# Rotary queries of two heads from one weight slot, and attention scores from split operands

## The chip, the cores and the metric

One core of a Trainium2 chip runs the whole program. The metric is the device time of one execution in microseconds; lower is better. The median of three runs of the kernel before is 3111.38 us (3108.11 to 3111.99).

## The reference, cut to what matters

Two transformer blocks run on 512 tokens of width 1024. The first has two layers (a feed-forward part, a mixing part, a second feed-forward part, a gated projection), the second has one. The change touches only the attention branch of the mixing part of the first block, which has 8 heads in each of the 2 layers:

```python
q = (rmsnorm(q_c, q_norm_g) @ w_uq).reshape(b, s, 8, 128 + 64)     # from 384 columns
q_nope, q_rope = q[..., :128], apply_rope(q[..., 128:], cos, sin)
kv = (rmsnorm(kv_c, kv_norm_g) @ w_ukv).reshape(b, s, 8, 128 + 128) # from 256 columns
k_rope = apply_rope(k_r, cos, sin)                                  # one for all heads
# apply_rope: [x1*cos - x2*sin, x2*cos + x1*sin], halves of 32
# for each block of 128 queries, keys up to its end:
s = (q_nope @ k_nope.T + q_rope @ k_rope.T) * 192 ** -0.5           # chunk mask of 64
o = softmax(s) @ v
```

## The kernel before, in words

Activations lie transposed: features on the 128 partitions, the 512 tokens along the row. Every projection is cut into *weight slots*. A slot holds the weights for 128 output features, in K row tiles of 128x128; its result fills one of four PSUM banks (`proj`). PE reaches nearly full precision at the fast rate by splitting both operands into a rounded part and a remainder (`hi`, `lo`, type fp32r) and multiplying hi x hi, hi x lo and lo x hi, so a slot costs 3K matmuls of 512 columns (`three`, L1042 to L1044; `slot_mm`). Each slot passes four engines: SP loads it into `raw`, ACT rounds it (`split_hi`, L617), DVE subtracts (`split_lo`, L1477), PE multiplies, and DVE or ACT evacuates the bank. The splits run `AHEAD` = 2 slots ahead; the ring has `RING` = 4 places. Semaphores count slots: `slot_done` by PE, `slot_read` by whoever evacuates; PE may refill a bank once `slot_read` has reached it.

The order of work on each engine is written out by hand, and each engine works in its program order; PE's order is the one in which slots are numbered. In a layer the stages are: feed-forward, `lora` (6 slots), `conv` (12), `gates` (12), `head0` (the 4 slots of head 0), `gates_end` (4), `heads` (4 slots for each of heads 1 to 7), `branch_out`, `mix_out`, feed-forward, `ple`.

A head has four slots: content queries (K = 3), rotary queries (K = 3), keys (K = 2), values (K = 2). The weights of the rotary slot hold the 64 rotary columns twice, the second time with swapped halves; DVE multiplies its bank by a table of cosines and sines (`cs`), and the fold of the two halves is done in the keys' rotary operand `work(15)`, so that a contraction over 128 rows gives the rotated product. DVE copies the other three banks (`head_evac`, L1596 and L1598).

The period of a head, `core`, has the attention of head n and the slots of head n+1 interleaved. PE does: `turn(3)` (transposes of the probabilities, 4 tiles), `scores(1)`, slot 0, `turn(2)`, `scores(0)`, slot 1, `turn(1)`, slots 2 and 3, `turn(0)`; then `enter` for head n+1 (`scores(3)`, `scores(2)`, four transposes of v), then the product with v (`ot`, L1161). `scores(qt)` makes one block of 128 queries against (qt+1) x 128 keys: a plain f32 matmul for content (L1110), an fp32r matmul of 128 columns that adds the chunk mask (L1111), a plain f32 one for the rotary part (L1112). The trace records a plain f32 matmul as two. DVE takes the row maximum (L1606) and scales it (L1609), ACT takes the exponential with the row sum (`exp`, L679), DVE scales the row by the sum's reciprocal (`row_norm`, L1615 and L1618), PE transposes it (`turn`, L1122), ACT copies it (`copy_pt`, L707). At the end ACT and DVE split the head's output (L701, L1654). Head 7 has the first four slots of `branch_out` in place of a next head's. `enter` waits first for `slot_read` to reach the next head's last slot less one, later for the last one itself. GpSimd is idle in this stage; its sums of squares (`squares`, L530 to L535) come in the stages around it.

Of the kernel before, what the change touches and what calls it, by code (L numbers as in the profile page):

```python
# [26 lines left out]
P = 128  # L27
# [39 lines left out]
HEAD_TILES = [Q_LORA // P, Q_LORA // P, KV_LORA // P, KV_LORA // P]  # L67
_stage("gates", [KD] * 12)
_stage("head0", HEAD_TILES)
_stage("gates_end", [KD] * 4)  # L70
_stage("heads", HEAD_TILES * (HEADS - 1))
# [72 lines left out]
def build(nc, I, out_t):  # L144
    ctx = ExitStack()
    with ctx:
# [35 lines left out]
        work_t, _ = place("work", 16 * S)  # L182
        sq_t, _ = place("sq", S)
        acc_t, _ = place("acc", S)
        rs_t, _ = place("rs", S)
# [15 lines left out]
        vec0 = modc[:, 0:KD]  # L201
        small2 = stat_t[:, 32:64]
# [70 lines left out]
        v_turned, v_ready = sem("v_turned"), sem("v_ready")  # L273
# [118 lines left out]
        def _(sp):  # L392
# [51 lines left out]
            with sp.Fori(0, DEPTH) as layer:  # L444
# [6 lines left out]
                def head(s0, i):  # L451
                    for j in range(2):
                        load(Slot(layer, s0 + j, i, 4), I["head_q"][layer, (i if s0 == STAGE["head0"] else i + 1) * 2 + j])
                    for j in range(2):
                        load(Slot(layer, s0 + 2 + j, i, 4), I["head_kv"][layer, (i if s0 == STAGE["head0"] else i + 1) * 2 + j])
                head(STAGE["head0"], 0)
                loads(layer, "gates_end", 4, lambda i: I["in_w"][layer, i + 30])
                with sp.Fori(0, HEADS - 1) as i:
                    head(STAGE["heads"], i)
# [41 lines left out]
        def _(pool):  # L501
# [7 lines left out]
            pool.memset(cmask[0:64, 64:P], NEG).then_inc(consts_ready, 1)  # L509
# [103 lines left out]
        def _(act):  # L613
# [96 lines left out]
            with act.Fori(0, DEPTH) as layer:  # L710
# [10 lines left out]
                for j in range(12):  # L721
# [8 lines left out]
                    if j >= 3 and j < 8:  # L730
                        act.wait_ge(lora_norm, 5 * layer + j - 2)
                        act.activation(a_hi(j - 3), work(j - 3), ACT.Copy).then_inc(lora_hi, 1)
                    if j % 3 == 2:
# [24 lines left out]
                s0 = STAGE["heads"] + AHEAD  # L758

                def heads(it):  # L760
                    end = isinstance(it, int)
                    for q in range(2):
                        core(layer, 2 * it + q, [Slot(layer, s0 + 4 * q + j + (24 if end else 0), 0 if end else it, 8) for j in range(4)],
                             end and q == 1)
                with act.Fori(0, HEADS // 2 - 1) as it:
                    heads(it)
                heads(HEADS // 2 - 1)
# [272 lines left out]
        def _(pe):  # L1040
# [65 lines left out]
            def scores(n, q, qt):  # L1106
# [33 lines left out]
            def core(layer, hd, q, slots, end):  # L1140
# [10 lines left out]
                if not end:  # L1151
                    run[3]()
# [1153 lines left out]
```

## Time and profile before

| | |
|---|---|
| median of 3 runs | 3111.38 us (3108.11 to 3111.99) |
| the profiled execution | 3112.69 us, of which the span from first to last instruction is 3110.9 |
| PE busy | 3043.7 us, 98% of the span, 13548 matmuls |
| PE weight load busy | 2449.6 us |
| DVE busy | 1725.1 us, 55% |
| ACT busy | 1058.1 us, 34% |
| GpSimd busy | 291.2 us, 9% |
| mean granted TensorE clock | 0.989 |

Busy shares are over the whole span. A matmul's duration holds the latency of the pipeline, and consecutive ones overlap, so what a matmul costs is read from the distance of starts. ACT's and DVE's operations overlap a little as well. The rows for the stage of the heads stand in the section on rows.

### The profile page before, as it was taken

The page shows a single profiled execution, that of the slowest core. Times are in us where ns is not written, and L with a number is a line of the kernel's source. Part 1 is how long each engine was busy: PE and PEld are TensorE (multiplying, and loading weights), DVE is VectorE, ACT ScalarE, POOL GpSimd, SP SyncE. Part 2 cuts the span into 40 slices and gives each one's busy share as a digit, 9 for nine tenths or more (in the row PEclk, how much of TensorE's full clock was granted, in tenths as well). Part 3 has the DMA queues.
Part 4 walks back from the last instruction along what each step waited for, and adds up shares of the span by engine and source line. Part 5 has one row for each costly group of instructions (what it writes and reads, how often), then busy time and mean ns, then how long its engine had stood idle before and what let it go on. Part 6 is the DMA issues. An engine that isn't in the chain of part 4 may idle for free. (4 is left out here: it accounts for less than half of the span.)

```text
span 3110.9 us, 39289 instructions
## 1 busy us (share of the span) xinstructions
PE 3043.7 (98%) x13548; PEld 2449.6 (79%) x13548; DVE 1725.1 (55%) x2469; ACT 1058.1 (34%) x1628; POOL 291.2 (9%) x236
## 2 busy tenths in 40 slices
PE   7999999999999999999999999999999799989999
PEld 6888888778888887888878877888888675678887
DVE  6555564565655556555456465555556767453334
ACT  4222323332332235322232333232223545552223
POOL 1000200000200023000020000200003214600000
PEclk9999999999999999999999999999999899999999
DMA  5232222113323222432232212333222420112222
GB/s 185 88 143 96 94 95 77 61 52 116 142 95 138 99 84 87 152 139 95 88 107 83 78 42 80 110 144 135 99 88 86 149 75 21 37 65 97 100 94 81
DMA packets 87965, 303.18 MB, mean 97 GB/s; under 512 B 10400, under 2 KB 20768, under 8 KB 86688
## 3 DMA queue, kind: packets, MB, share of 16 engines
q1 hardware_dynamic: 87840, 301.59, 27.7%
q8 instruction: 69, 1.13, 0.1%
q14 instruction: 56, 0.46, 0.0%
HBM read 299.45 MB, written 2.10 MB: 97 GB/s over the span
## 5 line engine op out<-in xcount | busy, mean ns | idle before, releaser
L1042 PE MATMUL proj<-u_hi,w_hi 128*128 128x512 f32 x2616 | 1029.2, 393 | 29.0 <-DVE u_lo L1482 23.0
L1043 PE MATMUL proj<-u_lo,w_hi 128*128 128x512 f32 x2616 | 1020.8, 390 | 0.0
L1044 PE MATMUL proj<-u_hi,w_lo 128*128 128x512 f32 x2616 | 1020.8, 390 | 0.0
L1477 DVE TENSOR_TENSOR w_lo<-raw,w_hi 128x1024 fp32r<-128x1024 f32 (+4 forms) x575 | 659.1, 1149 | 487.5 <-ACT w_hi L617 479.7
L617 ACT ACTIVATE w_hi<-raw 128x1024 fp32r<-128x1024 f32 (+4 forms) x575 | 538.7, 948 | 357.8 <-PE proj L1044 233.5
L1042 PEld LDWEIGHTS proj<-u_hi,w_hi 128*128 128x128 f32 x2616 | 492.7, 188 | 141.8 <-DVE u_lo L1482 28.5
L1043 PEld LDWEIGHTS proj<-u_lo,w_hi 128*128 128x128 f32 x2616 | 493.1, 188 | 104.4 <-issue 3.4
L1044 PEld LDWEIGHTS proj<-u_hi,w_lo 128*128 128x128 f32 x2616 | 492.9, 188 | 103.0
L1042 PE MATMUL proj<-a_hi,w_hi 128*128 128x512 f32 x960 | 380.8, 397 | 1.6 <-DVE a_lo L1787 0.9
L1044 PE MATMUL proj<-a_hi,w_lo 128*128 128x512 f32 x960 | 374.3, 390 | 0.0
L1043 PE MATMUL proj<-a_lo,w_hi 128*128 128x512 f32 x960 | 373.8, 389 | 0.0
L1493 DVE TENSOR_TENSOR work<-proj,rs 128x512 f32<-128x512 f32 x260 | 179.4, 690 | 304.3 <-PE proj L1044 304.1
L1042 PEld LDWEIGHTS proj<-a_hi,w_hi 128*128 128x128 f32 x960 | 180.3, 188 | 41.0 <-issue 2.6
L1044 PEld LDWEIGHTS proj<-a_hi,w_lo 128*128 128x128 f32 x960 | 180.2, 188 | 38.2
L1043 PEld LDWEIGHTS proj<-a_lo,w_hi 128*128 128x128 f32 x960 | 180.4, 188 | 36.1
L659 ACT ACTIVATE a_hi<-work 128x512 f32 (+1 forms) x88 | 55.6, 632 | 441.4 <-DVE work L1548 441.4
L530 POOL TENSOR_TENSOR acc<-h 128x512 f32<-128x512 f32 x6 | 6.2, 1040 | 2088.7 <-DVE h L1566 1321.3
L1566 DVE SCALAR_TENSOR_TENSOR h<-proj,h 128x512 f32<-128x512 f32 x96 | 66.3, 690 | 165.6 <-PE proj L1044 165.4
L656 ACT ACTIVATE work<-work 128x512 f32<-128x512 f32 x88 | 55.6, 632 | 266.0 <-DVE work L1493 266.0
L1551 DVE TENSOR_TENSOR a_lo<-work,a_hi 128x512 f32 (+1 forms) x88 | 61.0, 693 | 80.9 <-ACT a_hi L659 80.9
L623 ACT ACTIVATE u_hi<-h,vec 128x512 fp32r<-128x512 f32 x48 | 34.8, 725 | 141.2 <-DVE h L1566 82.2
L535 POOL TENSOR_TENSOR acc<-acc,sq 128x512 f32<-128x512 f32 x42 | 67.6, 1609 | 3.3
(410 smaller groups left out, 2826.7 us busy)
## 6 DMA issues: line engine op xcount, KB each, us to landing
raw<-in_ffn_gu SPq DMA_DIRECT2D x174, 512.0 KB, 3.5
raw<-in_in_w SPq DMA_DIRECT2D x68, 512.0 KB, 3.5
raw<-in_ffn_dn SPq DMA_DIRECT2D x64, 512.0 KB, 3.5
raw<-in_ff SPq DMA_DIRECT2D x64, 512.0 KB, 3.5
gate<-in_ada SPq DMA_DIRECT2D x8, 3072.0 KB, 11.5
raw<-in_ffn_dn SPq DMA_DIRECT2D x32, 384.0 KB, 3.0
raw<-in_in SPq DMA_DIRECT2D x18, 512.0 KB, 3.5
raw<-in_mla_out SPq DMA_DIRECT2D x16, 512.0 KB, 3.5
```

The lines of the kernel that those rows point to most:

```text
L535: pool.tensor_tensor(acc, acc, sq, ALU.add).then_inc(sum_ready, 1)
L617: act.activation(wt(w_hi, slot, slot.tiles), wt(raw, slot, slot.tiles), ACT.Copy)\
L623: act.activation(u_hi(m), h(m), ACT.Copy, scale=gain[:, m:m + 1]).then_inc(u_hi_ready, 1)
L656: act.activation(work(2 + q), work(q), ACT.Tanh, scale=0.5).then_inc(tanh_ready, 1)
L659: act.activation(a_hi_t[:, bass.ds((2 * it + q) * S, S)], work(8 + q), ACT.Copy)\
L1042: pe.matmul(out, w_h, x_h, start=first, stop=False)
L1043: pe.matmul(out, w_h, x_l, start=False, stop=False)
L1044: return pe.matmul(out, w_l, x_h, start=False, stop=last)
L1477: dve.tensor_tensor(wt(w_lo, slot, slot.tiles), wt(raw, slot, slot.tiles), wt(w_hi, slot, slot.tiles).bitcast(F32), ALU.subtract).then_inc ...
L1493: return dve.tensor_tensor(dst, proj[:, slot.pos, :], rs, ALU.mult)
L1551: dve.tensor_tensor(a_lo_t[:, at], work(8 + q), a_hi_t[:, at].bitcast(F32), ALU.subtract)\
L1566: dve.scalar_tensor_tensor(at, proj[:, slot.pos, :], 0.25, at, ALU.mult, ALU.add)\
```

## The change

Rotary weights are laid out with the 64 rotary columns of two heads side by side, once, in a new array `head_r`, and a slot of kind `r` gives the rotary queries of a pair. It comes with the slots of heads 0, 2, 4 and 6 (`HEAD_SLOTS`, `CORE_SLOTS`): in `head0`, and in the periods of heads 0, 2 and 4, which so have 4 slots, the others 3. The rotation is done after the projection. ACT copies the bank in four pieces of 32 rows with the halves of each head exchanged (`head_slot`, kind `r`); DVE multiplies the bank by the cosines; GpSimd multiplies the exchanged copy by the sines and adds the two. In the next period (for the first pair, in `gates_end`) ACT rounds one head's 64 rows of it and DVE writes the remainder into the other 64 rows of the same tile (`rot_hi`, `rot_lo`), once for each head of the pair.

Content queries and keys are split as they leave the bank: ACT writes the rounded part, DVE the remainder. ACT, no longer DVE, copies v. Keys carry the factor -192**-0.5, so the sign of the scores is turned: DVE takes the row minimum and no longer scales it, and the mask's constant changes sign. The rotary keys are split as well, after the last `conv` slot and no longer after its second. Scores are six fp32r matmuls: three for content, the mask, one rotary matmul over 128 rows (both parts of the queries stacked, against rounded keys) and one over 64 rows (rounded queries against the keys' remainder). `row_norm(0)` and the evacuation of the third slot change places on DVE. The loops over pairs of heads are written out on all engines. Places change: cosines and sines of all 128 rows lie in `acc` and `sq`, the rounded queries of odd heads in `rs`.

```diff
-HEAD_TILES = [Q_LORA // P, Q_LORA // P, KV_LORA // P, KV_LORA // P]
+HEAD_SLOTS = [("r", 0), ("q", 0), ("k", 0), ("v", 0)]
+CORE_SLOTS = [[("q", hd + 1), ("k", hd + 1)] + ([("r", hd // 2 + 1)] if hd in (0, 2, 4) else []) + [("v", hd + 1)]
+              for hd in range(HEADS - 1)]
+CORE_AT = [sum(len(c) for c in CORE_SLOTS[:hd]) for hd in range(HEADS)]
+HEAD_TILES = {"r": Q_LORA // P, "q": Q_LORA // P, "k": KV_LORA // P, "v": KV_LORA // P}
...
+        q_hi, q_lo = (lambda q: rs_r[:, :] if q else split_tile(0)), (lambda q: u_lo(7) if q else split_tile(8))
+        k_hi, k_lo = split_tile(4), split_tile(5)
+        kr_hi, kr_lo = split_tile(15), split_tile(1)
+        rot_q = lambda q: split_tile(2 + q)
+        v_tok = lambda q: ux(7) if q else work(7)
+        cos2, sin2 = acc, sq
+        turned_q = lambda p: (ux(6), ux(14)) if p else (work(11), work(12))
+        hi_rows = lambda q: slice(64 * q, 64 * q + 64)
+        lo_rows = lambda q: slice(64 - 64 * q, 128 - 64 * q)
+        ROT = 10
...
+                    if e == 1:
+                        for p in range(HEADS // 2):
+                            straight, crossed = turned_q(p)
+                            step = ROT * (HEADS // 2 * layer + p)
+                            pool.wait_ge(rope_step, step + 4)
+                            pool.tensor_tensor(crossed, crossed, sin2, ALU.mult).then_inc(rope_step, 1)
+                            pool.wait_ge(slot_read, Slot(layer, STAGE["heads"] + CORE_AT[2 * p - 2] + 2 if p else STAGE["head0"]).done)
+                            pool.wait_ge(rope_step, step + 5)
+                            pool.tensor_tensor(straight, straight, crossed, ALU.add).then_inc(rope_step, 1)
...
-                               ACT.Exp, bias=stat_t[:, 8 + qt:9 + qt], scale=SCALE1,
+                               ACT.Exp, bias=stat_t[:, 8 + qt:9 + qt], scale=-1.0,
                                accum_out=stat_t[:, 16 + qt:17 + qt]).then_inc(exp_ready, 1)
 
-            def core(layer, hd, slots, end):
+            def head_slot(layer, slot, kind, i):
+                q = i % 2
+                if kind == "v":
+                    act.wait_ge(slot_read, slot.done - 1)
+                act.wait_ge(slot_done, slot.done)
+                bank = proj[:, slot.pos, :]
+                if kind == "q":
+                    act.activation(q_hi(q), bank, ACT.Copy).then_inc(qk_hi_ready, 1)
+                elif kind == "k":
+                    act.activation(k_hi, bank, ACT.Copy, scale=-SCALE1).then_inc(qk_hi_ready, 1)
+                elif kind == "v":
+                    act.activation(work(6), bank, ACT.Copy).then_inc(slot_read, 1)
+                else:
+                    for r in range(4):
+                        to, of = slice(32 * r, 32 * r + 32), slice(32 * (r ^ 1), 32 * (r ^ 1) + 32)
+                        act.activation(turned_q(i)[1][to, :], bank[of, :], ACT.Copy).then_inc(rope_step, 1)
+
+            def rot_hi(layer, p, q):
+                act.wait_ge(rope_step, ROT * (HEADS // 2 * layer + p) + 6 + 2 * q)
+                act.activation(rot_q(q)[hi_rows(q), :], turned_q(p)[0][hi_rows(q), :], ACT.Copy).then_inc(rope_step, 1)
+
+            def core(layer, hd, slots, ahead, end):
 
                 n = layer * HEADS + hd
-                split = lambda j: split_hi(slots[j])
+                do = lambda kind: [head_slot(layer, slots[j], *c) for j, c in enumerate(CORE_SLOTS[hd]) if c[0] == kind]
+                turn_next = not end and hd % 2 and hd < HEADS - 1
                 copy_pt(n, 3)
                 exp(n, 1)
-                split(0)
+                split_hi(ahead[0])
+                if turn_next:
+                    rot_hi(layer, hd // 2 + 1, 0)
+                if not end:
+                    do("q")
                 copy_pt(n, 2)
                 exp(n, 0)
-                split(1)
+                split_hi(ahead[1])
+                if turn_next:
+                    rot_hi(layer, hd // 2 + 1, 1)
+                if not end:
+                    do("k")
                 copy_pt(n, 1)
-                split(2)
-                split(3)
+                split_hi(ahead[2])
+                if not end:
+                    do("r")
+                if len(ahead) > 3:
+                    split_hi(ahead[3])
+                if not end:
+                    do("v")
...
+                    head_slot(layer, Slot(layer, STAGE["head0"] + j), *HEAD_SLOTS[j])
                 s0 = STAGE["gates_end"]
                 for j in range(4):
                     split_hi(Slot(layer, s0 + j + AHEAD))
+                    if j == 0:
+                        rot_hi(layer, 0, 0)
+                        rot_hi(layer, 0, 1)
...
-                pe.matmul(sc[:, qt % 2, 0:w], work(q)[:, qt * P:w], work(4 + q)[:, 0:w], start=True, stop=False)
+                pe.matmul(sc[:, qt % 2, 0:w], q_hi(q)[:, qt * P:w], k_hi[:, 0:w], start=True, stop=False)
+                pe.matmul(sc[:, qt % 2, 0:w], q_hi(q)[:, qt * P:w], k_lo[:, 0:w], start=False, stop=False)
+                pe.matmul(sc[:, qt % 2, 0:w], q_lo(q)[:, qt * P:w], k_hi[:, 0:w], start=False, stop=False)
                 pe.matmul(sc[:, qt % 2, qt * P:w], ident_r[:, :], cmask_r[:, :], start=False, stop=False)
-                pe.matmul(sc[:, qt % 2, 0:w], work(2 + q)[:, qt * P:w], work(15)[:, 0:w], start=False, stop=True)\
+                rows = hi_rows(q)
+                pe.matmul(sc[:, qt % 2, 0:w], rot_q(q)[:, qt * P:w], kr_hi[:, 0:w], start=False, stop=False)
+                pe.matmul(sc[:, qt % 2, 0:w], rot_q(q)[rows, qt * P:w], kr_lo[rows, 0:w], start=False, stop=True)\
...
+                pe.wait_ge(rope_step, ROT * (HEADS // 2 * layer + hd // 2) + 8 + 2 * q)
...
-            def head_evac(slot, j, q):
-                evac(slot, work((0, 2, 4, 6)[j] + (q if j < 3 else 0)), cs if j == 1 else None)
-
-            def row_max(n, qt):
+            def head_slot(layer, slot, kind, i):
+                bank = proj[:, slot.pos, :]
+                n = layer * HEADS + i
+                if kind == "q":
+                    dve.wait_ge(qk_hi_ready, 2 * n + 1)
+                    dve.tensor_tensor(q_lo(i % 2), bank, q_hi(i % 2).bitcast(F32), ALU.subtract).then_inc(slot_read, 1)
+                elif kind == "k":
+                    dve.wait_ge(qk_hi_ready, 2 * n + 2)
+                    dve.scalar_tensor_tensor(k_lo, bank, -SCALE1, k_hi.bitcast(F32), ALU.mult, ALU.subtract).then_inc(slot_read, 1)
+                elif kind == "r":
+                    dve.wait_ge(rope_step, ROT * (HEADS // 2 * layer + i) + 4)
+                    dve.tensor_tensor(turned_q(i)[0], bank, cos2, ALU.mult).then_inc(slot_read, 1)
+
+            def rot_lo(layer, p, q):
+                dve.wait_ge(rope_step, ROT * (HEADS // 2 * layer + p) + 7 + 2 * q)
+                turned = turned_q(p)[0][hi_rows(q), :]
+                dve.tensor_tensor(rot_q(q)[lo_rows(q), :], turned, rot_q(q)[hi_rows(q), :].bitcast(F32), ALU.subtract)\
+                   .then_inc(rope_step, 1)
+
+            def row_min(n, qt):
                 i = n * QT + QT - qt
                 dve.wait_ge(s_done, i)
-                dve.tensor_reduce(stat_t[:, 4 + qt:5 + qt], sc[:, qt % 2, 0:(qt + 1) * P], AX, ALU.max)\
-                   .then_inc(mx_ready, 1)
-                dve.wait_ge(mx_ready, i)
-                dve.tensor_scalar(stat_t[:, 8 + qt:9 + qt], stat_t[:, 4 + qt:5 + qt], -SCALE1, None, ALU.mult)\
...
+                dve.tensor_reduce(stat_t[:, 8 + qt:9 + qt], sc[:, qt % 2, 0:(qt + 1) * P], AX, ALU.min)\
...
-                def side(j):
-                    split_lo(ahead[j])
+                turn_next = not end and hd % 2
+
+                def do(kind, j):
                     if end:
                         gated(layer, slots[j], 2 * j, gate(2 * j))
-                    else:
-                        head_evac(slots[j], j, 1 - q)
-                row_max(n, 1)
-                side(0)
-                row_max(n, 0)
+                    for s, c in zip(slots, () if end else CORE_SLOTS[hd]):
+                        if c[0] == kind:
+                            head_slot(layer, s, *c)
+                row_min(n, 1)
+                split_lo(ahead[0])
+                if turn_next:
+                    rot_lo(layer, hd // 2 + 1, 0)
+                do("q", 0)
+                row_min(n, 0)
                 row_norm(n, 1)
-                side(1)
-                side(2)
+                split_lo(ahead[1])
+                if turn_next:
+                    rot_lo(layer, hd // 2 + 1, 1)
+                do("k", 1)
                 row_norm(n, 0)
-                side(3)
-                if not end:
-                    enter(n + 1, 1 - q)
+                split_lo(ahead[2])
+                do("r", 2)
+                if len(ahead) > 3:
+                    split_lo(ahead[3])
+                if end:
+                    do("v", 3)
+                else:
+                    enter(n + 1, (hd + 1) % 2)
...
-                        dve.tensor_copy(work(15), sc[:, 0, :]).then_inc(kr_ready, 1)
-                    side(j)
+                        dve.tensor_scalar(kr_hi, sc[:, 0, :], -SCALE1, None, ALU.mult).then_inc(kr_ready, 1)
+                        dve.wait_ge(kr_ready, 2 * layer + 1)
+                        dve.scalar_tensor_tensor(kr_lo, sc[:, 0, :], -SCALE1, kr_hi.bitcast(F32), ALU.mult, ALU.subtract)\
...
+    o["head_r"] = stack(lambda l: slots_of(head_w(l)[:, :, NOPE:].reshape(Q_LORA, -1)))
```

## Rows read from the trace of the kernel before

**Rows 1.** The page: the span, and busy time of each engine.
```profile
span 3110.9 us, 39289 instructions
...
PE 3043.7 (98%) x13548; PEld 2449.6 (79%) x13548; DVE 1725.1 (55%) x2469; ACT 1058.1 (34%) x1628; POOL 291.2 (9%) x236
```

**Rows 2.** Windows: from:to, length, busy time by engine, clock; one head.
```profile
613.57:629.14 15.57, 15.57 (x74) 11.49 (x73) 10.21 (x27) 6.15 (x17) 0.00 (x0) 1.00 0.15 42
```

**Rows 3.** PE in order of time, one head: start, us, line, operation.
```profile
607.64 1.12 PE L1110 MATMUL sc<-work 128*128 128x512 f32 x2
...
609.57 0.81 PE L1110 MATMUL sc<-work 128*128 128x384 f32 x2
...
610.97 0.60 PE L1134 MATMUL tr<-ident,work 128*128 128x128 f32 x4
...
613.57 0.60 PE L1122 MATMUL tr<-ident,work 128*128 128x128 f32 x4
614.00 0.60 PE L1110 MATMUL sc<-work 128*128 128x256 f32 x2
...
615.21 0.39 PE L1043 MATMUL proj<-a_lo,w_hi 128*128 128x512 f32 x1
...
616.82 0.40 PE L1044 MATMUL proj<-a_hi,w_lo 128*128 128x512 f32 x1
617.05 0.49 PE L1122 MATMUL tr<-ident,work 128*128 128x128 f32 x3
617.38 0.39 PE L1110 MATMUL sc<-work 128*128 128x128 f32 x2
...
618.17 0.40 PE L1043 MATMUL proj<-a_lo,w_hi 128*128 128x512 f32 x1
```

**Rows 4.** ACT in order of time, the same head.
```profile
613.86 0.60 ACT L701 ACTIVATE u_hi<-ot 128x512 f32 x1 [1.24 <-PE ot L1161]
614.36 0.59 ACT L707 ACTIVATE work<-tr 128x512 f32<-128x512 f32 x1
...
616.34 0.41 ACT L617 ACTIVATE w_hi<-raw 128x256 fp32r<-128x256 f32 x1
```

**Rows 5.** DVE in order of time, the same head.
```profile
615.23 0.42 DVE L1606 TENSOR_REDUCE row_stats<-sc 128x1 f32<-128x256 f32 x1
...
617.26 0.69 DVE L1596 COPY work<-proj 128x512 f32<-128x512 f32 x1
...
618.76 0.35 DVE L1618 TENSOR_SCALAR work<-work,row_stats 128x256 f32<-128x256 f32 x1
...
622.64 0.29 DVE L1618 TENSOR_SCALAR work<-work,row_stats 128x128 f32<-128x128 f32 x1
```

**Rows 6.** Groups by form, ACT: copies out of PSUM at two widths.
```profile
L707 ACT ACTIVATE work<-tr 128x512 f32<-128x512 f32 x16 | 9.5, 593 | 0.5 <-ACT gate L752 0.5
...
L707 ACT ACTIVATE work<-tr 128x128 f32<-128x128 f32 x16 | 4.4, 277 | 27.9 <-PE tr L1122 27.9
```

**Rows 7.** Groups, PE: transposes of the probabilities, idle time before them.
```profile
L1122 PE MATMUL tr<-ident,work 128*128 128x128 f32 x160 | 28.5, 276 | 2.4 <-DVE work L1618 2.4
```

**Rows 8.** GpSimd by form, then DVE and GpSimd together in time.
```profile
L533 POOL TENSOR_TENSOR sq<-h 128x512 f32<-128x512 f32 x42 | 58.7, 1397 | 75.3 <-DVE h L1772 41.0 <-DVE h L1566 34.3
...
L535 POOL TENSOR_TENSOR acc<-acc,sq 128x512 f32<-128x512 f32 x42 | 67.6, 1609 | 3.3
...
379.76 1.29 POOL L535 TENSOR_TENSOR acc<-acc,sq 128x512 f32<-128x512 f32 x1
...
379.87 2.27 DVE L1477 TENSOR_TENSOR w_lo<-raw,w_hi 128x1024 fp32r<-128x1024 f32 x1 [1.08 <-ACT w_hi L617]
...
388.96 1.22 DVE L1477 TENSOR_TENSOR w_lo<-raw,w_hi 128x1024 fp32r<-128x1024 f32 x1 [4.12 <-ACT w_hi L617]
```

**Rows 9.** Windows at the start of the second layer.
```profile
1222.00:1225.00 3.00, 1.35 (x6) 0.78 (x5) 2.08 (x4) 2.24 (x4) 0.00 (x0) 1.00 0.67 243
...
1228.00:1231.00 3.00, 1.82 (x4) 0.83 (x3) 2.67 (x3) 3.00 (x5) 2.92 (x2) 0.50 0.28 108
```

More of the change, by code:

```diff
@@ L181, in build @@
         ax_t, _ = place("ax", 18 * S, at=a_at)
[L182 to L185, printed above, removed]
+        work_t, work_at = place("work", 16 * S)
+        work_r, _ = place("work_split", 16 * S, F32R, at=work_at)
+        sq_t, sq_at = place("sq", S)
+        acc_t, acc_at = place("acc", S)
+        rs_t, rs_at = place("rs", S)
+        rs_r, _ = place("rs_split", S, F32R, at=rs_at)
         cs_t, _ = place("rope_table", S)
@@ L449, in _ @@
                 loads(layer, "gates", 12, lambda i: I["in_w"][layer, i + 18])
[L451 to L456, printed above, removed]
+                head_w = lambda kind, i: I[{"q": "head_q", "r": "head_r", "k": "head_kv", "v": "head_kv"}[kind]][
+                    layer, i if kind in "qr" else 2 * i + (kind == "v")]
+                for j, (kind, i) in enumerate(HEAD_SLOTS):
+                    load(Slot(layer, STAGE["head0"] + j), head_w(kind, i))
                 loads(layer, "gates_end", 4, lambda i: I["in_w"][layer, i + 30])
-                with sp.Fori(0, HEADS - 1) as i:
-                    head(STAGE["heads"], i)
+                for j, (kind, i) in enumerate(sum(CORE_SLOTS, [])):
+                    load(Slot(layer, STAGE["heads"] + j), head_w(kind, i))
                 for s, (br, m) in enumerate(OUT_ORDER):
@@ L507, in _ @@
             pool.wait_ge(consts_ready, 5)
[L509 removed]
+            pool.memset(cmask[0:64, 64:P], -NEG).then_inc(consts_ready, 1)
             pool.affine_select(out=ident[:, :], in_=ident[:, :], compare_op=ALU.not_equal, fill=1.0, base=0,
@@ L732, in _ @@
                         act.activation(a_hi(j - 3), work(j - 3), ACT.Copy).then_inc(lora_hi, 1)
+                    if j == 9:
+                        for rows in (slice(0, 64), slice(64, P)):
+                            act.activation(cos2[rows, :], cs[0:64, :], ACT.Copy)
+                            act.activation(sin2[rows, :], cs[64:P, :], ACT.Copy)
                     if j % 3 == 2:
@@ L756, in _ @@
                 act.wait_ge(gate_tanh, 16 * (layer + 1) + 2)
[L758 to L767, printed above, removed]
+                s0 = STAGE["heads"]
+                for hd in range(HEADS):
+                    end = hd == HEADS - 1
+                    at = range(s0 + CORE_AT[hd], s0 + CORE_AT[hd] + (4 if end else len(CORE_SLOTS[hd])))
+                    core(layer, hd, [Slot(layer, s) for s in at], [Slot(layer, s + AHEAD) for s in at], end)
                 s0 = STAGE["branch_out"]
@@ L1141, in core @@
                 n = layer * HEADS + hd
-                run = [lambda s=s, j=j: slot_mm(s, conv_of if end else lora_of(j)) for j, s in enumerate(slots)]
+                run = [lambda s=s, j=j: slot_mm(s, conv_of if end else lora_of(CORE_SLOTS[hd][j][0])) for j, s in enumerate(slots)]
                 turn(n, 3)
@@ L1150, in core @@
                 run[2]()
-                if not end:
+                if not end and len(run) > 3:
                     run[3]()
@@ L1156, in core @@
                 else:
-                    enter(layer, hd + 1, 1 - q, slots[3].done)
+                    enter(layer, hd + 1, 1 - q, slots[-1].done)
                 pe.wait_ge(pt_ready, n * QT + QT + 1)
@@ L1160, in core @@
                 for k in range(QT):
-                    mm = pe.matmul(ot[:, k * P:S], work(7 + q)[:, k * P:(k + 1) * P], work(11 + k)[:, k * P:S],
+                    mm = pe.matmul(ot[:, k * P:S], v_tok(q)[:, k * P:(k + 1) * P], work(11 + k)[:, k * P:S],
                                    start=k == 0, stop=True, skip_group_check=True)
@@ L1199, in _ @@
                 s0 = STAGE["heads"]
-                with pe.Fori(0, HEADS // 2 - 1) as it:
-                    for q in range(2):
-                        core(layer, 2 * it + q, q, [Slot(layer, s0 + 4 * q + j, it, 8) for j in range(4)], False)
-                core(layer, HEADS - 2, 0, [Slot(layer, s0 + 24 + j) for j in range(4)], False)
+                for hd in range(HEADS - 1):
+                    core(layer, hd, hd % 2, [Slot(layer, s0 + CORE_AT[hd] + j) for j in range(len(CORE_SLOTS[hd]))], False)
                 s0 = STAGE["branch_out"]
@@ L1730, in _ @@
                     split_lo(Slot(layer, s0 + j + AHEAD))
-                    head_evac(Slot(layer, s0 + j), j, 0)
+                    head_slot(layer, Slot(layer, s0 + j), *HEAD_SLOTS[j])
+                dve.wait_ge(slot_read, Slot(layer, s0 + 3).done)
                 s0 = STAGE["gates_end"]
@@ L1734, in _ @@
                     split_lo(Slot(layer, s0 + j + AHEAD))
+                    if j == 0:
+                        rot_lo(layer, 0, 0)
+                        rot_lo(layer, 0, 1)
                     dve.wait_ge(gate_tanh, 16 * layer + 12 + j + 1)
@@ L1739, in _ @@
                 s0 = STAGE["heads"]
-                def heads(it):
-                    end = isinstance(it, int)
-                    for q in range(2):
-                        o = s0 + 4 * q + (24 if end else 0)
-                        r = 0 if end else it
-                        core(layer, 2 * it + q, q, [Slot(layer, o + j, r, 8) for j in range(4)],
-                             [Slot(layer, o + j + AHEAD, r, 8) for j in range(4)], end and q == 1)
-                with dve.Fori(0, HEADS // 2 - 1) as it:
-                    heads(it)
-                heads(HEADS // 2 - 1)
+                for hd in range(HEADS):
+                    end = hd == HEADS - 1
+                    at = range(s0 + CORE_AT[hd], s0 + CORE_AT[hd] + (4 if end else len(CORE_SLOTS[hd])))
+                    core(layer, hd, [Slot(layer, s) for s in at], [Slot(layer, s + AHEAD) for s in at], end)
                 s0 = STAGE["branch_out"]
```

36 lines of the change are left out of this document (18 added, 18 removed).

## The prediction

> **What bounds the kernel now.** I read the page first: the span is 3110.9 us and PE is busy 3043.7 us of it, DVE 55%, ACT 34% [rows 1]. So time goes where PE's instruction stream goes, unless another engine makes PE wait. Then the windows view of one head's period of the attention stage: 15.57 us, PE busy in all of it, DVE for 10.21, ACT for 6.15, clock 1.00 [rows 2]. The reader is to see no PE gap there: a matmul less is time less, as long as the two other engines keep up. Third, PE in order of time over that period [rows 3], read by starts, since a duration holds a pipeline's latency: from the second to the ninth matmul of a weight slot there are 7 steps from 615.21 to 616.82, 0.230 us each. The first of a run starts early, so I place it 0.23 before the second. Fourth, ACT and DVE over the same period [rows 4, 5], as both work in program order and this change leans on both.
>
> **What is removed from PE.** Weight slots first. Before, each head has a rotary slot of 3 row tiles with the 64 columns doubled; afterwards one serves two heads: 4 slots fewer in a layer, 4 x 3 tiles x 3 matmuls x 2 layers = 72 matmuls x 0.230 = **16.6 us**.
>
> Scores next. The old content and rotary matmuls are plain f32, recorded as two each. A group lasts 609.57 - 607.64 = 1.93 us at width 512, 610.97 - 609.57 = 1.40 at 384, 614.98 - 614.00 = 0.98 at 256 and 617.94 - 617.38 = 0.56 at 128 [rows 3]: 4.87 in a head. The two f32 matmuls of 512 and the mask in 1.93 us cost about 0.9 each, four slot matmuls. Afterwards there are five split ones and the mask. At 512 I take 5 x 0.23 and 0.11 for the mask, 1.26. At 384, 5 x 0.17 + 0.11 = 0.96. Below that the row of width 128 sets the floor: five matmuls in 0.56 is 0.112 each, as four transposes take 614.00 - 613.57 = 0.43, 0.108 each; the streaming of 128 columns is shorter, so what is left is the load of the weights. Six matmuls x 0.112 = 0.67 both at 256 and at 128, where the group becomes 0.11 *longer*. Sum 3.56, a gain of 1.31 per head, x 16 = **21.0 us**. Could a narrow split matmul run at the slow f32 rate? At 128 columns that would be 0.21; the four f32 records around the mask need 4 x 0.107, which leaves 0.14 for the mask, itself a split matmul of 128. So no; as a bound it would cost 5 x (0.21 - 0.11) + 5 x (0.43 - 0.11) = 2.1 per head. The page "TensorE: Matmul & The Clock Gate" of the Trainium skill, section Back-to-back issue gap, states about 81 ns per matmul at 128 columns. The rows show 112; by that page the two narrow groups would cost 0.49 each, 5.8 us less in all.
>
> **What waits instead.** I replay the three kinds of period with times from the start of the four transposes of qt 3 (613.57 in the trace). PE: transposes to 0.43, scores to 1.10, q slot to 3.16, transposes, scores to 4.2, k slot to 5.57, two transposes. ACT copies of 512 from PSUM last 0.60 and follow each other at 0.50 [rows 4, 6]; DVE's of 512 last 0.69 and follow at 0.61; DVE or ACT starts 0.21 after a slot's last step (617.26 after 617.05) [rows 3, 5]; an engine that waits for the other starts 0.04 later, PE 0.08 later.
>
> *Heads 0, 2 and 4 (q, k, r, v).* The r slot ends at 7.87. ACT makes four copies of 32 rows with crossed halves, 8.08 to 8.08 + 3 x 0.50 + 0.60 = 10.18. Behind it queue a weight split and the copy of v. DVE's product with the cosine waits for the fourth copy: 10.22 to 10.91. PE's entry into the next head waits for that product, since the slot count that stands for k is counted behind it: 10.99. PE is there at 9.47. Stall 1.5 us, x 6 = **9.1 us**. The v copy then ends near 11.5, before PE has done the two score groups (13.2), so it adds nothing. What are 32 rows worth? The nearest rows are 128x512 in 593 ns and 128x128 in 277 ns, the latter as many elements as 32x512 [rows 6]. Both have all rows, so length is what they vary, and I take 0.60. At 0.28 the four take 0.8, stall 0.2, 7.8 us less over all. The page "ScalarE: Activation LUTs" of the Trainium skill, section What ACT_TABLE_LOAD costs, gives one element per cycle and lane, 186 ns + 0.833 ns per element: 613 ns whatever the rows, a stall of 1.6. No row here has 32 partitions.
>
> *Heads 1, 3 and 5 (q, k, v, and the rotated pair is split).* The row minimum of qt 1 ends at 2.08 as now (615.23 + 0.42), since the output's split ahead of it stays. ACT in order: exp to 2.60, weight split (0.41) to 3.0, rotary copy 2.9 to 3.55, q_hi 3.45 to 4.05, transposed copy to 4.44. DVE: rotary remainder 3.6 to 4.3, q_lo 4.2 to 4.9, row minimum to 5.06, row scaling to 5.52. PE wants that at 5.57: just met. ACT: exp 5.10, weight split to 5.92, second rotary copy to 6.45, k_hi 6.35 to 6.95. DVE: weight split 5.96 to 6.52, second remainder 6.5 to 7.2, k_lo 7.1 to 7.8, reciprocal, scaling to 8.16. PE has the last transpose due at 9.24 - 2.06 = 7.18 and gets it at 8.24. Stall 1.1, x 6 = **6.6 us**.
>
> *Head 6.* The same without the rotated pair: scaling at 7.5, stall 0.4, x 2 = **0.8 us**.
>
> *Head 7.* Now DVE scales the last row tile after the third slot's evacuation, and PE waits for it: 2.4 us over the two layers [rows 7], all the idle time ahead of these transposes. The change moves the scaling ahead of it. The 2.4 goes; next late is the third slot itself, which PE has done. Gain **2.4 us**.
>
> *First head and the last gate slots.* From the start of the r slot, v is due at 24 x 0.23 = 5.5 and the first gate slot at 6.9. Four crossed copies 2.27 to 4.37, weight split of v to 4.7. GpSimd's product starts at 4.4 and lasts 1.4, its sum 1.6 [rows 8]. While GpSimd added, a DVE subtraction of two SBUF tiles that began 0.11 us later took 2.27 instead of 1.22 us [rows 8], done 1.0 after GpSimd's end. So v's remainder waits to 5.8, ends 6.3, and the gate slot's 1024 wide one waits for the sum, to 7.5 + 1.2: PE starts the gate slot 1.8 late. x 2 = **3.6 us**; without the collision 0.6 each. The weight remainder is on no critical path in the other periods.
>
> Costed at nothing: the four cosine and sine copies in conv (ACT 34% busy there), the split of the keys' rotary part (PE is 14 slots away), the DMA queue (fewer slots and no more bytes; each load waits for a weight split as before), the loops written out (PE shows no gap at the old loop's turn). The small scaling of the row maximum leaves the chain of a score, where PE had cover.
>
> **Sum.** 16.6 + 21.0 + 2.4 = 40.0 less of PE's work and waits; 9.1 + 6.6 + 0.8 + 3.6 = 20.1 of new waits; net 19.9. The profiled execution took 3112.69 (span 3110.9 and 1.8 around it), so 3092.8. It lies 1.3 above the median of the runs, so **3091.5 us** there.
>
> **Rivals.** *Short copies* (0.28 per 32-row copy, shorter rotary copies): for it, equal element counts; against, nothing varies rows. 3091.5 - 7.8 = 3084, and 3080 if the rotary copies of 64 rows are shorter too. *PE hides all:* no stall, 3071; against it, slacks at the entry and at the last transpose are under 2 us. *More queueing:* the collision with GpSimd also falls on the periods, 1 us each in the six with an r slot and 0.5 in the rest: 3091.5 + 6 + 4 = 3101. *It eats its gain:* ACT and DVE, 72% and 68% of a 13.2 us period by my sums (ACT 6.15 + q, k, v, the rotary copy and half the crossed ones, 3.4; DVE 10.2 - 1.2), add a further 1.9 and 1.3 per period: 3091.5 + 11.4 + 8 = 3111. *Slower, by the clock:* at the entry after an r slot. If a crossed copy costs twice a plain one (1.2), that stall is 3.7 us. At the start of the second layer PE was busy 1.35 of 3 us, and six us later the granted clock was 0.50, 1.2 of 2.4 GHz, over that window [rows 9]. Nine us at that level give back 4.5 us each time: 6 x (2.2 + 4.5) = 40, 3131. [...]
>
> **How the numbers follow.** Chances: the forecast (3086 to 3098) 0.48; short copies 0.16; no stalls 0.06; more queueing 0.14; eats its gain 0.09; clock 0.07. The range 3075 to 3108 leaves most of the first tail (3071), half of "eats its gain" and the clock outside. A measurement tells 0.2%, 6.2 us. Faster: the first four cases, 0.84, less the edge, 0.83; same 0.09; slower 0.08.
>
> **What would show it.** Right: 72 fewer slot matmuls; score groups near 1.26, 0.96, 0.67 and 0.67; periods of 15.8, 13.3 and 12.6 us; PE idle ahead of the scores of width 512 by 1.5 us, releaser the DVE product; ahead of the last transpose by 1.1, releaser the row scaling; no idle time in head 7; the first gate slot 1.8 late. Wrong: crossed copies well under 0.6 us; a clock below 1.00 in the heads; a narrow split matmul over 0.12; stalls of other owners.

## The result and the profile after

The changed kernel takes 3125.01 us (median of 5 runs, 3124.29 to 3132.12) against 3111.38 for the kernel before; over all the runs the ratio is 1.0053, interval 1.0042 to 1.0064. It is 13.6 us slower, where 19.9 us less were forecast, and it lies outside the range of 3075 to 3108.

The page of the kernel after, its span and the first line of its busy times, answering to [rows 1]:

```profile
span 3122.4 us, 39135 instructions
...
PE 3040.5 (97%) x13540; PEld 2448.8 (78%) x13540; DVE 1713.3 (55%) x2391; ACT 1112.8 (36%) x1724; POOL 312.0 (10%) x252
```

PE's busy time fell by only 3.2 us while the span grew by 11.5. Nearly all that the change does happens between the first matmul of the first head's slots and the first matmul of head 7's output, in each layer: 156.45 us before and 162.83 after in the first layer, 156.51 and 166.07 in the second. That is +15.9; the rest of the program took 4.4 less in this profile, which is no effect of the change (see the account of the terms).

PE in order of time in one head after, answering to [rows 3]. The columns are start, duration, engine, line, operation; in brackets the idle time before it and who ended it:

```profile
605.34 0.31 PE L1173 MATMUL sc<-work_split,rs_split 128*128 128x128 f32 x1
605.48 0.28 PE L1174 MATMUL sc<-work_split,rs_split 128*128 128x128 f32 x1
605.59 0.28 PE L1175 MATMUL sc<-work_split,u_lo 128*128 128x128 f32 x1
605.70 0.27 PE L1176 MATMUL sc<-chunk_mask_r,ident_r 128*128 128x128 f32 x1
605.81 0.28 PE L1178 MATMUL sc<-work_split 128*128 128x128 f32 x1
606.02 0.32 PE L1179 MATMUL sc<-work_split 64*128 64x128 f32 x1
606.27 0.50 PE L1105 MATMUL proj<-a_hi,w_hi 128*128 128x512 f32 x1
...
610.26 0.33 PE L1189 MATMUL tr<-ident,work 128*128 128x128 f32 x1 [0.72 <-DVE work L1697]
610.44 0.50 PE L1173 MATMUL sc<-work_split 128*128 128x512 f32 x1
610.78 0.40 PE L1174 MATMUL sc<-work_split 128*128 128x512 f32 x1
611.01 0.40 PE L1175 MATMUL sc<-work_split 128*128 128x512 f32 x1
611.25 0.23 PE L1176 MATMUL sc<-chunk_mask_r,ident_r 128*128 128x128 f32 x1
611.31 0.45 PE L1178 MATMUL sc<-work_split 128*128 128x512 f32 x1
611.69 0.50 PE L1179 MATMUL sc<-work_split 64*128 64x512 f32 x1
612.12 0.44 PE L1173 MATMUL sc<-work_split 128*128 128x384 f32 x1
```

Read the starts. In the narrow group the first step takes 0.14 and the next three 0.11 each, near the forecast's 0.112. The step into the matmul with 64 rows (line 1179) takes 0.21 and the step out of it 0.25, and at width 512 they take 0.38 and 0.43 where two neighbours of 128 rows take 0.23. The four groups of a head last 1.68, 1.38, 1.19 and 1.04 us, 5.29 in all, against 4.87 before.

What PE waited for in the first layer's attention stage, all three lines, and the group of the transposes over the whole program, which answers to [rows 7]:

```profile
engine line waited for: us in total, times, longest us
PE sc L1173 <- DVE ux L1677: 5.8, 3, 1.9
PE tr L1189 <- DVE work L1697: 2.4, 4, 0.7
PE proj L1105 <- DVE w_lo L1543: 1.3, 2, 0.8
```

```profile
L1189 PE MATMUL tr<-ident,work 128*128 128x128 f32 x160 | 28.3, 275 | 4.7 <-DVE work L1697 4.7
```

These are the three waits that the prediction named: entry after the r slot (1.94 each), last transpose (0.72 in heads 1, 3 and 5, 0.20 in head 6), first head (0.84 and 0.51). The old wait of head 7 is gone; the 4.7 is all of the new heads.

The other engines at the entry, in order of time, answering to [rows 4, 5 and 8]:

```profile
592.41 2.43 ACT L723 ACTIVATE ux<-proj 32x512 f32<-32x512 f32 x4 [1.00 <-PE proj L1107]
...
594.87 0.69 DVE L1677 TENSOR_TENSOR ux<-proj,acc 128x512 f32<-128x512 f32 x1 [2.57 <-ACT ux L723]
594.92 1.27 POOL L571 TENSOR_TENSOR ux<-ux,sq 128x512 f32<-128x512 f32 x1 [37.77 <-ACT ux L723]
595.48 0.99 DVE L1543 TENSOR_TENSOR w_lo<-raw,w_hi 128x256 fp32r<-128x256 f32 x1
...
595.79 0.49 PE L1173 MATMUL sc<-work_split,rs_split 128*128 128x512 f32 x1 [1.94 <-DVE ux L1677]
```

The four crossed copies take 2.43 us. DVE's product then holds PE, and the weight remainder behind it takes 0.99 beside GpSimd instead of 0.42.

Last the windows (columns as in [rows 2]; the clock is the number after POOL's count), around the next such entry, and one in a later head for comparison:

```profile
620.00:625.00 5.00, 5.00 (x28) 4.14 (x27) 3.25 (x9) 3.08 (x9) 0.00 (x0) 1.00 0.26 72
625.00:630.00 5.00, 3.06 (x13) 1.97 (x11) 1.60 (x2) 3.44 (x7) 2.51 (x2) 0.93 0.09 26
630.00:635.00 5.00, 5.00 (x13) 3.32 (x13) 2.33 (x5) 1.45 (x4) 0.10 (x1) 0.50 0.13 39
635.00:640.00 5.00, 5.00 (x24) 3.65 (x23) 1.81 (x6) 2.03 (x6) 0.00 (x0) 0.88 0.00 0
...
660.00:665.00 5.00, 3.06 (x14) 2.12 (x12) 1.93 (x3) 3.54 (x7) 1.96 (x2) 1.00 0.12 39
```

After the gap of 1.94 us that ended at 628.28 the granted clock went to 0.50, that is 1.2 of 2.4 GHz, from about 629.3 to 636.2: by these windows 6.9 us (0.7, 5.0 and 1.2). PE was never idle in the window from 630 to 635, but the group of width 384 took 2.41 us there instead of 1.38. The gap that ended at 663.8 is as long, its window is as busy, and the clock stayed at 1.00. There are six gaps of this kind and three such drops, one in the first layer and two in the second. The period that holds the first takes 20.91 us (616.15 to 637.06), the same kind of period without one 17.84 (651.67 to 669.51): 3.07 each. Two of the five runs, 3130.9 and 3132.1 us, had a mean granted clock of 0.985 where the three near 3125 had 0.988, which two or three further drops would make (an estimate; only a run of the three has a trace).

| term | forecast | in the trace |
|---|---|---|
| slots, 72 matmuls fewer (936 records where there were 960 on each of three lines) | -16.6 | -16.6 |
| score groups | -21.0 | +6.7 (16 x 0.42) |
| head 7 | -2.4 | -2.4 |
| entry, heads 0, 2, 4 | +9.1 | +11.6 (6 x 1.94) |
| last transpose, heads 1, 3, 5 | +6.6 | +4.3 (6 x 0.72) |
| head 6 | +0.8 | +0.4 (2 x 0.20) |
| first head | +3.6 | +2.7 (2 x 1.35) |
| half clock after a gap | 0 | +9.2 (3 x 3.07) |
| attention stages | -19.9 | +15.9 |

The right column adds up to what the stages grew by, though its first line and the 3.07 are worked out from counts and one pair of periods. Two lines carry the miss: scores by 27.7 and the clock by 9.2.

### The profile page after: what moved, and what is told of

The parts are those of the page before. It is cut to its first block and busy times, and to the rows that moved or that the text cites. A ratio compares the mean times of both kernels' runs of the same rounds, so it can differ in the third digit from the quotient of the medians.

```text
span 3122.4 us, 39135 instructions
## 1 busy us (share of the span) xinstructions
PE 3040.5 (97%) x13540; PEld 2448.8 (78%) x13540; DVE 1713.3 (55%) x2391; ACT 1112.8 (36%) x1724; POOL 312.0 (10%) x252
## 5 line engine op out<-in xcount | busy, mean ns | idle before, releaser
L1105 PE MATMUL proj<-u_hi,w_hi 128*128 128x512 f32 x2616 | 1029.2, 393 | 29.5 <-DVE u_lo L1548 22.2
L1105 PE MATMUL proj<-a_hi,w_hi 128*128 128x512 f32 x936 | 370.5, 396 | 3.3 <-DVE w_lo L1543 1.7
L1107 PE MATMUL proj<-a_hi,w_lo 128*128 128x512 f32 x936 | 364.7, 390 | 0.0
L1106 PE MATMUL proj<-a_lo,w_hi 128*128 128x512 f32 x936 | 364.7, 390 | 0.0
```

The source lines that it names most:

```text
L1105: pe.matmul(out, w_h, x_h, start=first, stop=False)
L1106: pe.matmul(out, w_h, x_l, start=False, stop=False)
L1107: return pe.matmul(out, w_l, x_h, start=False, stop=last)
```

## The experiments

All of them start from the changed kernel. The kernel before took 3110.53 us beside the first four and 3109.05 beside the other three. Two questions are asked: is the cost of the 64-row matmul that of changing the number of rows, and do gap and clock hang together?

**All 128 rows for the keys' remainder.** The queries' two stacked parts meet the remainder, so one product that was left out before is added; all else stays.

```diff
-                rows = hi_rows(q)
-                pe.matmul(sc[:, qt % 2, 0:w], rot_q(q)[rows, qt * P:w], kr_lo[rows, 0:w], ...)
+                pe.matmul(sc[:, qt % 2, 0:w], rot_q(q)[:, qt * P:w], kr_lo[:, 0:w], ...)
```

> The matmul of the keys' remainder reads all 128 rows of the stacked queries, not 64. Theory R (the change of row count costs about 0.2 us ahead of it and 0.2 behind it): the four score groups fall from 1.68, 1.38, 1.19 and 1.04 us to 1.26, 0.96, 0.77 and 0.62, sum 3.6, which is 27 us less PE work; some comes back as longer waits of PE for DVE and ACT (the entries and last transposes come 0.8 us sooner in a period, so up to 12 us). Time 3125 - 15 to 27, near 3104. Rival N (the split matmuls of a score group cost what they cost, whatever the rows): groups and time unchanged, 3125. On the clock: if a gap of 1.9 us sets the dips, they stay, with gaps of 2.3 or more; if the 64-row matmuls do, they go.

Measured: 3099.98 us (3099.04 to 3100.47), 0.9963 of before, interval 0.9949 to 0.9978; 25.0 less than the changed kernel for the same count of matmuls. PE in order of time, then waits of the first layer's attention stage:

```profile
607.93 0.49 PE L1173 MATMUL sc<-work_split 128*128 128x512 f32 x1
...
608.78 0.45 PE L1177 MATMUL sc<-work_split 128*128 128x512 f32 x1
609.07 0.40 PE L1178 MATMUL sc<-work_split 128*128 128x512 f32 x1
609.30 0.33 PE L1173 MATMUL sc<-work_split 128*128 128x384 f32 x1
...
610.29 0.38 PE L1201 MATMUL tr<-ident,work 128*128 128x128 f32 x2
```

```profile
PE sc L1173 <- DVE ux L1676: 5.8, 3, 1.9
PE tr L1188 <- DVE work L1696: 3.4, 4, 1.0
```

The step out of the second rotary matmul is 0.23 now; the group of 512 lasts 1.37 instead of 1.68 and that of 384 0.99 instead of 1.38. So a matmul over twice the rows costs less time. The entry's wait is as before, not longer as expected. The last transpose waits 1.0 and no longer 0.7, since PE comes to it sooner. And the clock still falls, once in each layer, with no matmul of 64 rows left among the scores; windows of this kernel:

```profile
650.00:655.00 5.00, 3.06 (x14) 2.28 (x13) 2.36 (x5) 3.54 (x7) 1.52 (x2) 0.99 0.21 66
655.00:660.00 5.00, 5.00 (x19) 4.00 (x18) 2.37 (x5) 1.45 (x4) 1.09 (x1) 0.66 0.08 26
```

But each of these drops is only half as long: 3.4 us at half clock by the second window, and likewise in the second layer. The period that holds one takes 18.00 us instead of 16.40, so the two cost 3.1 us together, where the changed kernel's three cost 9.2.

**An earlier entry, 64 rows kept.** PE enters the next head once the count that stands for k has come, not the r slot's product behind it.

```diff
-                pe.wait_ge(slot_read, last - 1)
+                pe.wait_ge(slot_read, last - behind)    # behind = len(slots) - 2
```

> In the periods with an r slot PE's entry waits for the count that stands for k, not for the one after it that stands for r; the score matmuls keep their 64 rows. Theory S (the stall of 1.94 us at six entries is the queue of four crossed copies and the cosine product, and the clock dips follow from it): the stall goes, 11.6 us, and with it the three dips, 9 us: time 3125 - 21 = 3104 or a little above, as DVE reaches the row minimum late. Rival (another wait ends at about the same time, v's evacuation or the row minimum): PE stalls one step later, at v's transposes or the next period's first transposes, by 1 to 2 us, and the time stays above 3115.

Measured: 3103.70 us (3101.76 to 3106.09), 0.9979 of before, interval 0.9969 to 0.9989; 21.3 less than the changed kernel. The waits hold no line of the entry any more:

```profile
PE tr L1189 <- DVE work L1697: 2.3, 4, 0.7
PE proj L1105 <- DVE w_lo L1543: 1.4, 2, 0.8
```

The entry's waits were 11.6, so 9.7 more went with them; the granted clock is 1.00 in every window of the heads. That is about the 9.2 of the table: the half clock came with the gap.

**Both edits.**

> Both edits. If the two costs are independent: 3125 - 27 - 21 = 3077, plus what DVE and ACT now fail to keep up with: the last transposes of heads 1, 3, 5 wait 1.1 to 1.3 instead of 0.7 (+3 us), and the period after an r slot waits at its first transposes by 0.5 to 1 (+3 to 6). Near 3085. Rival (ACT and DVE bound the stage, so that each edit alone takes the whole gain): not below 3100.

Measured: 3086.52 us (3085.58 to 3088.71), 0.9920 of before, interval 0.9903 to 0.9937. The single gains of 25.0 and 21.3 became 38.5 together, 7.8 less than their sum. The shorter time at half clock was counted in both (the first edit had brought it from 9.2 to 3.1, so 6.1 of it), and a new wait takes 1.4 in each layer: 8.9. The first two waits:

```profile
PE tr L1188 <- DVE work L1696: 3.4, 4, 1.0
PE tr L1201 <- ACT work L767: 1.4, 3, 0.5
```

The line of ACT is new: v's transposed row waits for its copy, 0.5 in each of three heads, once the entry is not late.

**Both edits and another order on ACT and DVE.** The row scaling goes ahead of the weight remainder and of k's, and the second split of the rotated pair behind the next weight split.

```diff
 (DVE)
+                row_norm(n, 0)
                 split_lo(ahead[1])
-                if turn_next:
-                    rot_lo(layer, hd // 2 + 1, 1)
                 do("k", 1)
-                row_norm(n, 0)
                 split_lo(ahead[2])
+                if turn_next:
+                    rot_lo(layer, hd // 2 + 1, 1)
 (ACT: rot_hi(layer, hd // 2 + 1, 1) moves behind split_hi(ahead[2]) likewise)
```

> As both edits, and in every period DVE scales the last row tile ahead of the key slot's split and evacuation, and the second head's rotary split of a pair comes after the keys on ACT and DVE. Theory: the wait at the last transposes is the queue of DVE ahead of that scaling: it goes, 0.7 to 1.3 us in each of 6 periods and 0.2 to 0.6 in 2, 6 to 9 us below both edits alone, near 3077. Rival (the same work only queues elsewhere: the keys' remainder is then late for the entry by as much): within 3 us of both edits alone.

Measured: 3078.82 us (3076.37 to 3079.94), 0.9895 of before, interval 0.9878 to 0.9911. It beats both kernels, the one before by some 32 us. The waits that are left:

```profile
PE tr L1201 <- ACT work L767: 1.4, 3, 0.5
PE proj L1105 <- DVE w_lo L1542: 1.4, 2, 0.8
```

The 3.4 ahead of the last transpose is gone in both layers (the second layer's waits are the same), 6.8 of the 7.7 measured. What was missing in the forecast's schedule was an order, not capacity.

**One copy of 128 rows instead of four crossed ones.** This leaves out the exchange of halves in the rotary queries.

```diff
-                    for r in range(4):
-                        to, of = slice(32 * r, 32 * r + 32), slice(32 * (r ^ 1), 32 * (r ^ 1) + 32)
-                        act.activation(turned_q(i)[1][to, :], bank[of, :], ACT.Copy).then_inc(rope_step, 1)
+                    act.activation(turned_q(i)[1], bank, ACT.Copy).then_inc(rope_step, 4)
```

> The changed kernel, but ACT copies the bank of an r slot once over all 128 rows and does not exchange the halves (so the rotation's second term is left out of its place). Theory S (PE's 1.94 us at six entries is the sum of the copies and the product): four copies took 2.43 us, one takes 0.60, so the stall falls to about 0.1 us and the clock dips go with it: 3125 - 11 - 9 = 3105, as with the entry's wait moved. If a copy went by its rows, one over 128 rows would take the place of four over 32 at the same time, the stall would stay and so would the time.

Measured: 3103.18 us (3101.28 to 3105.92), 0.9980 of before, interval 0.9970 to 0.9989. The waits:

```profile
PE tr L1187 <- DVE work L1695: 2.4, 4, 0.7
PE sc L1171 <- DVE ux L1675: 0.5, 3, 0.2
PE proj L1103 <- DVE w_lo L1541: 0.2, 1, 0.2
```

The entry waits 0.2 instead of 1.9 and the first head's wait all but goes; with gaps of 0.2 the clock is 1.00 throughout. So the entry's wait was the copies' time, and a second way to take the gap away takes the half clock away too.

**The mask on 64 rows as well.** From the earlier entry: the mask's matmul goes right ahead of the 64-row one, on the same rows (this leaves the mask out for half the heads). If each 64-row matmul is dear, 64 more of them cost 10 us and more; if the change of rows is, nothing.

```diff
+                rows = hi_rows(q)
                 pe.matmul(sc[:, qt % 2, 0:w], rot_q(q)[:, qt * P:w], kr_hi[:, 0:w], ...)
-                pe.matmul(sc[:, qt % 2, qt * P:w], ident_r[:, :], cmask_r[:, :], ...)
-                rows = hi_rows(q)
+                pe.matmul(sc[:, qt % 2, qt * P:w], ident_r[rows, :], cmask_r[rows, :], ...)
                 pe.matmul(sc[:, qt % 2, 0:w], rot_q(q)[rows, qt * P:w], kr_lo[rows, 0:w], ...)
```

> The kernel with the entry's wait moved and 64-row score matmuls, but the mask's matmul reads the same 64 rows and stands right ahead of the 64-row rotary one (for odd heads this leaves the mask out, as its nonzero rows are the other half). Theory T (what costs is each change between 128 and 64 rows, about 0.15 us in and 0.2 out): two changes in a group as before, so the groups and the time stay, 3104. Rival M (each 64-row matmul costs 0.35 more, by itself): 64 more of them, 22 us more, 3126.

Measured: 3103.45 us (3101.14 to 3106.03), 0.9979 of before, interval 0.9969 to 0.9988, against 3103.70 without this edit. PE in order of time:

```profile
608.97 0.40 PE L1177 MATMUL sc<-work_split 128*128 128x512 f32 x1
609.29 0.32 PE L1178 MATMUL sc<-chunk_mask_r,ident_r 64*128 64x128 f32 x1
609.46 0.45 PE L1179 MATMUL sc<-work_split 64*128 64x512 f32 x1
609.83 0.44 PE L1173 MATMUL sc<-work_split 128*128 128x384 f32 x1
```

The group lasts 1.66 (from 608.17), as 1.68 in the changed kernel, and the step between the two matmuls of 64 rows is 0.17. The number of changes is the same, and so is the price. The price is also the same for the lower 64 rows (even heads) and the upper ones (odd heads): all groups of width 384 at full clock in the changed kernel last 1.37 or 1.38. Why a change of rows costs time is not shown.

**The first head, one split further ahead.** From the best kernel: ACT and DVE split the weights of the head slots one slot earlier, so that v's remainder comes ahead of the r slot's product.

```diff
                 (ACT; DVE likewise with split_lo)
+                split_hi(Slot(layer, STAGE["head0"] + AHEAD))
                 for j in range(4):
-                    split_hi(Slot(layer, STAGE["head0"] + j + AHEAD))
+                    if j < 3:
+                        split_hi(Slot(layer, STAGE["head0"] + j + 1 + AHEAD))
                     head_slot(layer, Slot(layer, STAGE["head0"] + j), *HEAD_SLOTS[j])
```

> The fastest version so far, and in the stage of the first head ACT and DVE split one slot further ahead, so that the values' weights are split ahead of the crossed copies. Theory: PE's wait of 0.84 us for the values' weights goes; the next one, 0.51 us for the first gate slot's weights, shrinks or stays by GpSimd's collision with DVE's subtraction: 0.8 to 1.3 us a layer, 1.6 to 2.6 in all, 3078.8 to about 3076.7. Rival (the collision only moves to the wider split, 1.05 us long): no change.

Measured: 3079.85 us (3078.15 to 3080.95), 0.9905 of before, interval 0.9888 to 0.9922: no gain over 3078.82. The waits show where it went:

```profile
PE tr L1203 <- ACT work L767: 1.4, 3, 0.5
PE sc L1175 <- DVE work_split L1683: 0.8, 1, 0.8
PE proj L1107 <- DVE w_lo L1544: 0.2, 1, 0.2
```

The 1.4 ahead of the slots became 0.2 there and 0.8 ahead of the first scores, whose rounded queries' remainder now stands behind the earlier split. The wait moved with the work.

## Why the prediction was wrong, step by step

**Scores (-21.0): the step that failed.** It was the sum 5 x 0.23 + 0.11, which put the matmul of 64 rows at the price of one with 128, unasked: none of the rows that it read had fewer rows in a matmul, and neither a bound nor a rival stood for it. The prediction bounded the slow f32 rate instead, which did not come: the narrow steps of 0.11 show it (the Trainium skill, "TensorE: Matmul & The Clock Gate", section Back-to-back issue gap, says about 81 ns there; the trace keeps to 110, so the measurement decides, as it did for the row before). The change of row count costs 0.31, 0.39, 0.40 and 0.29 us in the four groups (with 64 rows 1.68, 1.38, 1.19 and 1.04; with 128 1.37, 0.99, 0.79 and 0.75): 1.39 a head, 22.2 over 16 heads. The all-rows kernel was 25.0 us faster, and its attention stages took 26.8 less; that holds 6.1 less lost to the clock and 2.0 more at the last transposes: 22.2 + 6.1 - 2.0 = 26.3. What is left of the miss, 5.4, is the size of plain steps: 3.90 a head with all rows against the 3.56 forecast.

The trace of before did hold such changes, in the attention of the second block:

```profile
2639.13 0.60 PE L1333 MATMUL tr<-ident,work 128*128 128x128 f32 x4
2639.66 1.13 PE L1324 MATMUL sc<-ax 64*128 64x512 f32 x4
```

The four transposes of 128 rows start 0.11 apart, the last at 2639.46; the step from it into the matmul of 64 rows takes 0.20. The operations are others, so this gives no price for the scores, but it was a row from which the question could be asked.

**The clock (1.00): wrong too, 9.2 us.** The sum put nothing on it. The rival "slower, by the clock" had the right place and the right order of events, a gap and then half clock, but it needed a stall of 3.7 us from crossed copies at twice the price of a plain one; they kept to 0.61, and a gap of 1.94 was enough in three of six cases. Its price of 4.5 a drop, from nine us at half clock, was 3.07, from 6.9. The kernels without the gap have no drop in the heads, whether the wait or the copies were cut, and the kernel with the gap and no 64-row matmul has two, half as long. So the drop hangs on the gap; why one gap of 1.94 us is followed by it and the next is not, and what sets its length, stays open.

**Entry of heads 0, 2 and 4 (1.5 each): place, owner and mechanism right, 1.94 in size.** The start distance of 0.50 between ACT's copies was taken from copies of 128 rows; the crossed ones of 32 rows follow at 0.61, so the last ends 2.43 after the first began, not 2.10. Each lasts as long as a copy of 128 rows, so the rival of short copies falls. The rule of the Trainium skill's page "ScalarE: Activation LUTs", section What ACT_TABLE_LOAD costs, that the price goes by the length of a row and not by the number of rows, is borne out (613 ns by the page, 2.43 / 4 = 0.61 here); the stall of 1.6 that it gave fell short only by the overlap of copies that did not come.

**Last transpose (1.1 and 0.4): right in place and owner, less in size,** 0.72 and 0.20, because PE came later to it: its own score groups were longer. Where they were short again it was 1.0, near the forecast.

**First head (1.8): 1.35.** The collision with GpSimd happened as [rows 8] had it, at 256 columns 0.99 instead of 0.42, and again at the gate slot's 1024: 1.71 instead of 1.22.

**Slots, head 7 and the edits costed at nothing: right.** The time of the other stages did not grow. Of the 4.4 us that they took less in this profile, 4.3 lie behind the second layer's heads, in code that the change does not touch (1188.7 us before, 1184.4 after): there the clock is at 0.50 for part of the time in every profile, and from 2390 to 2800 us its mean was 0.93 before and 0.95 after. Over the nine profiles of this document, before, after and the seven experiments, that last part takes 1184.4 to 1188.7 us. So a difference of 4 us between two profiles says nothing here about an edit, and that is why gains are read from medians of several runs or within the heads.

**The other rivals.** The kernel that the forecast described, if its rows are uniform, is the first experiment: 3100.0, still 8.5 above the 3091.5 forecast. By its trace that is plain steps (5.4), the clock (3.1) and a longer entry (2.5), less 1.6 at the first head and the last transposes: 9.4. The 3086.5 with both edits lies nearer only because it has no wait at the entry, which the forecast priced at 9.1; that nearness is chance. "More queueing" had the collision right (0.99 instead of 0.42 in the periods with an r slot), but no wait of PE in the heads is for it. "It eats its gain" had the worry of a lost gain right and the engines wrong: with the queue reordered ACT and DVE keep up but for 0.5 us at three entries a layer, and it was PE that became slower.

Not tried: letting DVE's product run beside ACT's crossed copies, which would take the entry's wait from its cause and not from its count.

## What to carry to other kernels

Before pricing a matmul by its columns, look whether its number of rows differs from its neighbours': filling the unused rows cost nothing here and saved 25 us, some 22 of them in the matmuls themselves. Where a wait is on a counter that several producers raise in order, ask whose count it takes, and move the slow producer behind the one that is needed: one number was worth 21 us. Price a gap on TensorE above its own length where it comes near two microseconds, since half the speed may follow it.

## What the runs showed of the hardware

- A matmul of 64 rows between matmuls of 128 costs 0.29 to 0.40 us more for the pair of changes (changed kernel against the first experiment), about the same at 128 and at 512 columns; two matmuls of 64 rows in succession cost it once (1.66 against 1.68 us a group).
- A gap of 1.94 us in an otherwise full TensorE was followed by about 7 us at clock 0.50 in three of six cases, and by about 3.4 us in two of six in the kernel with uniform rows; in the seven kernels whose longest wait there is 1.2 us or less, the one before among them, the clock stayed at 1.00 in the heads.
- Four ACT copies of 32 rows by 512 columns take 2.43 us, 0.61 from start to start with no overlap, where copies of 128 rows follow each other at 0.50 in [rows 4].
